# Another step order for the recurrence in a hybrid decoder kernel: two PSUM copies go to ScalarE, VectorE takes the next tile's blocks later

## What is computed

```python
def step(S, inp):
    r_t, w_t, k_t, v_t, kk_t, a_t = inp
    sa = jnp.einsum('bhvk,bhk->bhv', S, kk_t)
    S = S * w_t[:, :, None, :] - sa[..., None] * (kk_t * a_t)[:, :, None, :] + v_t[..., None] * k_t[:, :, None, :]
    return S, jnp.einsum('bhvk,bhk->bhv', S, r_t)

S_out, y = lax.scan(step, S_in.astype(F32), seq)
yn = _group_norm(y, C_HEADS, gn_g, gn_b, RWKV_GN_EPS)
bonus = jnp.sum(rh * kh * rk.reshape(C_HEADS, C_HEAD_DIM), -1, keepdims=True) * vh
out = (yn + bonus.reshape(B, L, C)) * g
```

## Time and profile before

| | before |
|---|---|
| median of 3 runs | 1114.13 us (1112.66 to 1115.87) |
| the profiled execution, its own time | 1119.49 us |
| its span in the profile | 1117.7 us |
| TensorE busy | 1007.3 us, 90% |
| VectorE busy | 501.9 us, 45% |
| ScalarE busy | 334.5 us, 30% |
| GpSimd busy | 128.1 us, 11% |
| mean granted clock of TensorE | 0.957 of full speed |

### The profile page before, as it was taken

The page is one execution under the profiler, slowest core; times in us unless marked ns, Lnnn a source line. Parts: engine busy times, 40 slices in busy tenths (PEclk is TensorE's granted clock), DMA queues, the critical chain, the costliest instruction groups (busy, mean ns, idle before and its releaser), DMA issues.

```text
span 1117.7 us, 25909 instructions
## 1 busy us (share of the span) xinstructions
PE 1007.3 (90%) x10538; PEld 652.7 (58%) x10538; DVE 501.9 (45%) x1265; ACT 334.5 (30%) x897; POOL 128.1 (11%) x152
## 2 busy tenths in 40 slices
PE   9999997599999499999878889899999948999995
PEld 3687454466665267777667777545655535666641
DVE  1581134322222546498646664766623352222217
ACT  0102114133333323323344342255422132333321
POOL 0010000210000300000222221411000011100013
PEclk9999998699999699999999999999999968999998
DMA  9752204999996631122322224494353089999935
GB/s 315 301 88 63 112 38 188 333 346 372 372 404 262 221 151 44 70 81 75 93 77 73 77 81 134 150 357 182 142 208 151 19 332 286 370 372 375 414 114 218
DMA packets 80864, 225.35 MB, mean 202 GB/s; under 512 B 9425, under 2 KB 50433, under 8 KB 62433
## 3 DMA queue, kind: packets, MB, share of 16 engines
q1 hardware_dynamic: 65184, 153.29, 37.9%
q0 software_dynamic: 11968, 57.71, 15.7%
q10 hardware_dynamic: 3584, 12.58, 3.0%
HBM read 201.57 MB, written 40.86 MB: 217 GB/s over the span
## 4 chain that ended last, share of the span: by engine, by line
PE 81%; DVE 7%; DMA 5%; issue 4%; ACT 2%; POOL 0%; DVEq 0%; SPq 0%; POOLq 0%; ACTq 0%
PE bank L1368 16%; PE bank L1272 10%; PE bank L1559 9%; PE bank L1392 8%; PE bank L1467 6%; PE bank L1493 3%; PE bank L1350 2%; PE bank L1669 2%; PE bank L1530 2%; PE bank L1964 1%; DMA xkept<-x 1%; DMA work<-xkept,idx 1%; PE bank L1989 1%; PE bank L1283 1%; DVE xT L2986 1%
## 5 line engine op out<-in xcount | busy, mean ns | idle before, releaser
L1272 PE MATMUL bank<-ring,cat 128*128 128x512 f32 x256 | 112.6, 594 | 1.3 <-ACT cat L2156 1.3
L1559 PE MATMUL bank<-xT,ring 128*128 128x288 f32 x448 | 110.9, 407 | 0.0
L1559 PEld LDWEIGHTS bank<-xT,ring 128*128 128x128 f32 x448 | 84.6, 190 | 23.8 <-issue 1.1
L1368 PE MATMUL bank<-ring,work 128*32 128x128 f32 (+1 forms) x1344 | 82.1, 316 | 1.7 <-DVE work L2619 1.7
L2629 DVE TENSOR_TENSOR work<-work,bank 128x192 f32<-128x192 f32 x32 | 11.3, 354 | 156.1 <-ACT work L2116 156.1
L1272 PEld LDWEIGHTS bank<-ring,cat 128*128 128x128 f32 x256 | 47.5, 190 | 57.2 <-issue 57.2
L2638 DVE COPY work<-bank 64x512 f32<-64x512 f32 x64 | 44.0, 687 | 67.2 <-PE bank L1392 66.7
L1368 PEld LDWEIGHTS bank<-ring,work 128*32 128x32 f32 (+1 forms) x1344 | 57.6, 121 | 24.7 <-issue 12.6
L1467 PE MATMUL bank<-xT,ring 128*128 128x288 f32 x256 | 63.1, 407 | 0.0
L2116 ACT ACTIVATE work<-bank 128x192 f32<-128x192 f32 x32 | 10.6, 331 | 162.1 <-PE bank L1368 162.1
L1467 PEld LDWEIGHTS bank<-xT,ring 128*128 128x128 f32 x256 | 48.3, 190 | 13.5 <-issue 0.4
(11 more groups left out here) (494 smaller groups left out, 1896.2 us busy)
## 6 DMA issues: line engine op xcount, KB each, us to landing
ring<-in_stream_dram SPq DMA_DIRECT2D x61, 1024.0 KB, 9.8
work<-in_stream_dram SPq DMA_DIRECT2D x16, 1024.0 KB, 18.2
cat<-in_stream_dram SPq DMA_DIRECT2D x16, 1024.0 KB, 20.4
by_batch<-in_pages_dram SPq DMA_DIRECT2D x128, 128.0 KB, 2.4
x<-in_stream_dram SPq DMA_DIRECT2D x12, 1024.0 KB, 19.2
xT<-in_stream_dram SPq DMA_DIRECT2D x12, 1024.0 KB, 17.8
yrows<-work ACTq DMA_DIRECT2D x32, 384.0 KB, 7.8
lnp<-in_ln_dram POOLq DMA_DIRECT2D x4, 1024.0 KB, 15.0
```

What stands on the lines that cost most here:

```text
L1272: i = pe.matmul(bank(n)[0:ROWS[tile], :], cat[:, k, tok(tile)], slot(w[k // 4], 4, 512)[:, k % 4, :], start=(k == 0), stop=(k == KC - 1))
L1368: i = pe.matmul(by_half[rows * q:rows * q + rows, :, to:to + width], xgT[:, e % 2, k, at:at + rows], w[:, :, width * q:width * q + width], ...
L1559: i = pe.matmul(bank(n + s)[:, 0:nn], slot(w, KC, 256)[:, k, P * (m % 2):P * (m % 2) + P], xT[:, k, a:a + nn], start=(k == 0), stop=(k == ...
```

## The change

X3 and H are copied by ScalarE in both halves. In the list of a tile, tokK moves from ahead of X3 to behind Y; tokB moves from ahead of HT to behind H; the rest of the group norm and the gate of the tile before move from behind Y to ahead of it. VectorE gets a list of its own, `DVE_RECURRENCE`, in which the next tile's bA stands behind H2T instead of ahead of it. The number of products and of banks is the same; the banks are numbered by the new order of the common list.

```diff
-BY_ACT = ("N2", "M2", "Y", "HT", "Z", "G2V")
-BY_BOTH = ("M4", "X2", "X3", "TT")
+BY_ACT = ("N2", "M2", "X3", "Y", "HT", "H", "Z", "G2V")
+BY_BOTH = ("M4", "X2", "TT")
...
-            + before("inv0", "inv1") + halves(t, "G2V") + [("tokK", t, 0)] + halves(t, "X3") + before("inv2", "inv3") + halves(t, "Y")
-            + before("scale", "gate") + [("tokB", t, 0)] + halves(t, "HT", "H") + after("bA") + halves(t, "H2T") + after("M")
+            + before("inv0", "inv1") + halves(t, "G2V", "X3") + before("inv2", "inv3", "scale", "gate") + halves(t, "Y")
+            + [("tokK", t, 0)] + halves(t, "HT", "H") + [("tokB", t, 0)] + after("bA") + halves(t, "H2T") + after("M")
...
+DVE_RECURRENCE = list(RECURRENCE)
+for t in range(1, NT):
+    for half in range(2):
+        DVE_RECURRENCE.remove(("bA", t, half))
+        DVE_RECURRENCE.insert(DVE_RECURRENCE.index(("H2T", t - 1, 1)) + 1 + half, ("bA", t, half))
...
-                for piece in RECURRENCE:
+                for piece in DVE_RECURRENCE:
                     (attention if piece[0] in ATT_JOBS else recurrence)(*piece)
...
-                    elif name == "H" or name in BY_BOTH and half == 1:
+                    elif name in BY_BOTH and half == 1:
```

## The result

The change makes the kernel slower: 1121.09 us median (1119.92 to 1124.92, 8 runs) against 1115.78 us for the kernel before in the same session (1112.66 to 1118.74, 8 runs), ratio 1.0051, 95% interval [1.0033, 1.0069]. Two repeats gave 1.0070 [1.0047, 1.0093] and 1.0047 [1.0020, 1.0074]; weighted by their intervals the three make 1.0056. The profiled execution took 1121.75 us, span 1119.9 us, mean granted clock 0.955. I had forecast 1116.2 and a range up to 1119.6, so both the size and the likeliest case were wrong. "Interval" in this text is always the 95% interval of a ratio, and "uncertain by" gives half the width of such an interval in microseconds.

A forecast was written before the change was run, and what follows sets the result against it. TensorE, nearly full, was taken as the bound, the second layer's recurrence as a back-and-forth chain. Tile terms 0.6 + 0 + 0.8 + 0.7 = +2.1 us on 1114.13 gave 1116.2 us, range 1111.8 to 1119.6.

The forecast's parts named there:

- low-clock stretches: TensorE at 1.2 instead of 2.4 GHz after idle time: 0.9 us each, two either way, not in the sum.
- stops: TensorE halting at "issue" with nothing to wait for; they may fall elsewhere, -3.0 to +1.5 us, not in the sum.
- rival 1: VectorE's backlog paid in full, 3.5 us, or 4.4 with one more low-clock stretch: 1118.5 us; chance 0.20.
- Step 1: Ahead of Y: X3 copied by ScalarE, tokK behind Y; Y starts near 624.2, a gain of 0.1 us.
- Step 2: Ahead of H2T: ScalarE copies H before tokB; H ready at 628.1 against 629.47, 1.4 us taken alone.
- Step 3: Ahead of tokB: it waits for the gate's bank until 628.88, so H2T starts 0.6 us later, at 630.4.
- Step 4: VectorE's bA behind H2T: its banks come free late, TT starts 1.0 us later, N2 at 635.25 against 634.33.
- The terms of the sum: Time added in the second layer's recurrence, tiles 0 to 3: 0.6, 0, 0.8 and 0.7 us, together +2.1.
- the bound of -1.0: Tile 1: -1.0 us if the 1.74 us stop ahead of Z goes and bA's end sets TT; forecast 0.
- Rival 2: Ahead of H2T and TT: bank waits do not matter, H2T, Z and TT 1.2 us earlier, -3.6: 1110.5; chance 0.06.
- Rival 3: Stops at "issue" and TensorE's clock turn to the good: -0.7 us, 1113.4, no difference; chance 0.12.
- Rival 4: The moved copies of X3 and H are dearer on ScalarE: about +6 us, 1120; chance 0.02.

The follow-up runs named there:

- after_third: The changed kernel run again with nothing altered, the second repeat: 1122.26 us, 1.0047 against the kernel before.
- f_order: The changed kernel, but with X3 and H copied as in the kernel before: 1120.42 us, 1.0049 against the kernel before.
- a_common: The changed kernel with VectorE back on the common list, bA ahead of I+H2T: 1120.56 us, 1.0030 against the kernel before.
- b_gate_ht: The changed kernel with the gate's product behind HT, VectorE's own list kept: 1117.4 us, 1.0018 against the kernel before.
- filled version: The changed kernel plus 44 unread identity products on TensorE in its two new waits: 1121.17 and 1118.88 us, 1.0026 and 1.0030 against the kernel before.
- c_both: The changed kernel with the gate's product behind HT and VectorE on the common list: 1117.04 us, 0.9991 against the kernel before; mean of three sessions 0.9987.

## Why the prediction was wrong

**The base.** The forecast of 1116.2 stood on a median of 1114.13 us from three executions of the kernel before. All eight of its session have 1115.78. So 1.65 us of the 4.9 us between 1116.2 and 1121.09 are the base, and the rest is the change itself: +2.1 forecast, +5.3 measured. Counted from 1115.78 the range would have reached 1121.3; that the measured time lies beyond it is the base's doing, and that it lies at the far end is the change's. Two ends of the range do not follow from their own terms either: the forecast less two low-clock stretches (1.8) and half of the stops (1.5) is 1112.9, not 1111.8, and rival 1 with one more stretch is 1119.4, not 1119.6.

**Step 1 (X3, tokK) was right.** Y starts at 622.70 + 1.50 = 624.20; I had said near 624.2.

**Step 2 (H is ready early) was right and worth nothing**, as said. ScalarE's four copies of HT and H are

```profile
625.21 1.20 ACT L2263 COPY ring<-bank 128x256 f32<-128x256 f32 x4
```

and end at 626.41, before the gate ends; with 1.50 us added that is 627.9, where I had 628.1.

**Step 3 (tokB waits for the gate's bank) was right in mechanism and place.** The gate ends at 626.98 + 1.50 = 628.48 (I had 628.52), tokB starts at 628.62 (I had 628.88). H2T starts at 631.30 where I had 630.4: tokB and bA run at the low clock (0.98 and 1.99 us, where the rows gave 0.66 and 1.05). In the two repeats, where the slow stretch comes later, H2T starts at 630.11 on the same scale (631.07 - 613.22 + 612.26 for after_third). The place of the bank wait was computed to a few tenths, the clock behind it was not.

**Step 4 (bA's backlog) was right.** TT is released by bA's last operation. N2 needs M's masked blocks; their last one, in the same timeline, is

```profile
634.20 0.42 DVE L2931 TENSOR_TENSOR xT<-bank,const 128x256 f32<-128x256 f32 x1
```

and ends at 634.62, 0.36 us before N2 starts at 634.98. The profile names the copy behind it (L2946), which N2 does not read. TT starts at 635.26 and UW at 636.96 (I had 633.95 and 635.9); again it is the low clock that adds. In both repeats TT starts at 633.68 and UW at 635.77 on the scale of before, within 0.3 us of the forecast.

**The terms of the sum**, from the lengths of the tiles in the two profiles of the kernel before and the three of the changed one:

| tile | before, two profiles | after, three profiles | term | forecast |
|---|---|---|---|---|
| 0 | 25.40, 25.60 | 26.85, 26.60, 26.90 | +1.3 | +0.6 |
| 1 | 31.40, 32.06 | 30.05, 31.10, 30.90 | -1.0 | 0 |
| 2 | 29.90, 29.65 | 31.40, 29.80, 29.70 | +0.5 | +0.8 |
| 3 | 27.30, 27.39 | 29.80, 30.10, 28.20 | +2.0 | +0.7 |

Tile 0 was under-priced: its TT waits 1.50 us for bA (1.03 us for Z's copies before), and the stop at "issue" ahead of EQ is 1.29 us against 1.02. Another 0.35 us are its first product, 1.90 us long instead of 1.55. I had put the backlog only ahead of N2 there. In tile 1 the 1.74 us stop of the earlier trace rows is gone (0.55 us ahead of Z in this profile), near the bound of -1.0 that I gave. Tile 2's 31.40 has a stop of 1.41 us at "issue" that the other two do not have. Together the four tiles took 117.1 us in the mean against 114.35: +2.8 us where I had 2.1. The measured loss is 5.3 us and more, so the profiles show only about half of it in these tiles.

**The step that failed is "the change leaves about as much idle time in each tile as before, so I take no difference" for the clock.** The amount of idle time was indeed not much larger: tile 2 had 1.03 + 1.33 + 1.03 + 0.34 = 3.7 us of it in the earlier trace rows, and has 0.41 + 1.78 + 1.54 + 0.52 = 4.3 us in the timeline above. But its two longest pieces are longer, 1.78 and 1.54 us against 1.33 and 1.03. A low-clock stretch stands in tile 3 in three of the four profiles that have both waits without spare work in them (the changed kernel's three and f_order's) and in none of the 14 others, among them those of a_common and b_gate_ht, which have one wait each. Whether it is the length of the pieces or the time added to them was not tried. Over whole executions the mean clock is 0.952 against 0.956: at half speed in the low stretches, that is 9.6% of 1119 us against 8.8% of 1116, 107 against 98 us. About 3 us of the loss go with it, by the filled version, which has the clock of the kernel before. The other half is what the filled version still loses, 1.0028 or 3.1 us: the waits themselves, that is my sum of 2.1 us with the term of tile 0 put right (+1.3 where I had +0.6), and whatever the spare products cost where they outlast a wait (0.3 us ahead of tokB in tile 2).

**The rivals.** Rival 1 (backlog paid in full and one more low-clock stretch, +4.4) was nearest, and with the stretch at its measured 1.6 us instead of 0.9 it would have read 5.1, against 5.3 to 6.6 measured. I gave it 0.20 because the stops at "issue" had covered the backlog in tile 1; they do, but only there. Rival 2 fell with the two waits in the profile; its mechanism is what c_both has, though the 3.6 us that I gave it come out as about 1.5, not clear of zero. Rival 3 fell: the clock went the other way. Rival 4, the dearer copies, fell in the rows (the changed kernel's ScalarE still takes 0.65 us for a pair of copies, where VectorE took 0.75), and c_both, with the same copies, is no slower than the kernel before. That is where the Trainium skill's rule, page "ScalarE: Activation LUTs", section "Rules for kernel authors", was weighed; its factor of about three is given for bf16, and for these fp32 copies out of banks the rows do not show VectorE to be the faster one. The hint of its page "Perfetto Trace Analysis", section "Optimization Strategy", that repeated idle stretches can mean too few buffers in the banks, the trace bears out in part: the two idle stretches that recur are waits for banks. But the number of banks was not what had to change: with the same eight, the gate's product behind HT, so that tokB gets another bank, and bA's banks handed back earlier, 7.7 us came back.

**What stays open.** The prompt tiles of the profiles show about 3 us of the loss with one to two low-clock stretches more, and no profile shows where the other half falls; the granted clock of the timed executions is known only as a mean, so how much of the 9 us more at the low clock lies in these tiles isn't settled. Nor is the cause of the stops at "issue". For the one behind UW in tile 2 the profiles do show when it comes: in all 11 profiles without spare products in which UW took 1.10 us there is a stop of 0.9 to 1.7 us, and in the four in which UW ran at the low clock (1.96 to 2.01 us: the earlier trace rows, both repeats of the change, b_gate_ht) there is none. A low-clock stretch there takes the place of the stop, which fits that it cost almost nothing in tile 2, and 1.6 us in tile 3, where the profiles show no such stop behind UW. The prediction put the two down as separate unseen costs.

## What to carry to other kernels

When pieces are moved in a hand-written order that also numbers the banks, look up for every moved piece which job had its bank eight numbers earlier and who empties it: a copy that is ready 1.4 us earlier was worth nothing here, since the piece ahead of its reader had got the bank of a slow elementwise chain. Price a wait not only by its length. Here two new waits seem to have cost about as much again in clock, so ask of each new wait whether an independent product can stand in it. A filler helped where low-clock stretches had followed the waits (1.0056 to 1.0028, hardly clear of scatter), and it cost time where they had not (0.9984 to 1.0003). And take the base of a forecast from more than three executions where single ones scatter by 15 us: 1.65 us of this miss were the base.

## What the runs showed of the hardware

- A wait that TensorE has for a bank alone (tokB for the gate, TT for bA) ended 0.14 us after VectorE's last operation; one for an operand that VectorE had just written took 0.36 us (N2 for M, above; H2T for H in the earlier trace rows). I had used 0.36 for tokB too, which put it 0.26 us late in the forecast. Why they differ wasn't tried.
- Work that nobody reads raised the clock: 44 spare products, mean clock 0.957 instead of 0.952 on the same chip, and 1.7 us less in the means, uncertain by 2.8 us (1.0056 to 1.0028 over all sessions).
- One stretch at the low clock cost tile 3 1.6 us (29.80 against 28.20 us for the same kernel) and tile 2 0.1 us (29.78 against 29.65 us for the kernel before), where the profile without it has a stop of 1.68 us at "issue" instead.
- Within one kernel, an execution whose mean clock was 0.001 lower was 0.6 us longer (179 executions, correlation -0.72).
